# Block products of the MLPs in another order, modulation sums in PSUM, weights two passes ahead

## The reference

```python
h = rmsnorm(x, norm_mlp[l]) * (1.0 + sc2) + sh2
ff = square(relu(h @ mlp_w1[l])) @ mlp_w2[l]      # 1024 -> 4096 -> 1024
x = x + g2 * ff
```

## Time and profile before

| | |
|---|---|
| median of 3 runs | 2931.09 us |
| profiled execution | 2930.64 us, span 2928.8 us |
| busy: TensorE, VectorE, POOL, ScalarE | 88%, 65%, 47%, 38% |
| mean granted TensorE clock | 0.943 |
| layer 0's MLP, passes 0 to 30 | 605.1 to 1530.2 us |
| layer 1's MLP, passes 32 to 62 | 2033.8 to 2870.9 us |

### The profile page before, as it was taken

How to read it: one execution, slowest core, us unless ns; L and a number is a source line. 1 busy time by engine, 2 the same in 40 slices (tenths; PEclk the granted TensorE clock), 3 DMA queues, 4 the chain that set the end, 5 groups by cost and what they waited for, 6 DMA issues and landing times. The chain is left out here.

```text
span 2928.8 us, 42150 instructions
## 1 busy us (share of the span) xinstructions
PE 2571.2 (88%) x13962; PEld 2462.9 (84%) x13962; DVE 1915.5 (65%) x2837; ACT 1113.4 (38%) x1884; POOL 1372.3 (47%) x907
## 2 busy tenths in 40 slices
PE   8999998978887896799997988878899996799997
PEld 4999998978787896799996877678899996699997
DVE  5876877367677764777775677765643443777775
ACT  5332333243333334333334454423444433433334
POOL 1211211244554454777772322334466664577772
PEclk9999999989999998899998999989999998899998
DMA  6422223214434435433332111132222235433332
GB/s 234 134 85 58 74 81 114 95 38 162 153 138 145 141 138 201 139 117 116 116 115 97 36 36 36 32 111 77 78 106 90 112 116 196 150 122 113 115 119 94
DMA packets 245983, 324.24 MB, mean 111 GB/s; under 512 B 14710, under 2 KB 221046, under 8 KB 239863
## 3 DMA queue, kind: packets, MB, share of 16 engines
q1 hardware_dynamic: 242436, 303.31, 31.0%
q10 hardware_dynamic: 3442, 19.65, 1.7%
HBM read 242.16 MB, written 80.75 MB: 110 GB/s over the span
## 5 line engine op out<-in xcount | busy, mean ns | idle before, releaser
L1086 PE MATMUL psum<-early_hi,unit_hi 128*128 128x384 f32 (+1 forms) x1408 | 507.0, 360 | 145.1 <-DVE part_x L1876 57.5
L1086 PE MATMUL psum<-late_hi,unit_hi 128*128 128x384 f32 x1408 | 485.1, 345 | 80.2 <-DVE x L1978 58.9
L787 POOL TENSOR_TENSOR unit_lo<-wide_raw,unit_hi 128x512 fp32r<-128x512 f32 x256 | 383.3, 1501 | 290.3 <-ACT unit_hi L1391 290.3
L1086 PE MATMUL psum<-early_lo,unit_hi 128*128 128x384 f32 (+1 forms) x1408 | 497.2, 353 | 0.0
L1086 PE MATMUL psum<-early_hi,unit_lo 128*128 128x384 f32 (+1 forms) x1408 | 496.2, 352 | 0.0
L1086 PE MATMUL psum<-late_lo,unit_hi 128*128 128x384 f32 x1408 | 480.6, 341 | 0.0
L1086 PE MATMUL psum<-late_hi,unit_lo 128*128 128x384 f32 x1408 | 480.3, 341 | 0.0
L1086 PEld LDWEIGHTS psum<-early_hi,unit_hi 128*128 128x128 f32 x1408 | 282.4, 201 | 163.2 <-DVE part_x L1876 62.0
L787 POOL TENSOR_TENSOR unit_lo<-unit_sum_s,unit_hi 128x512 fp32r<-128x512 f32 x256 | 375.0, 1475 | 61.1 <-ACT unit_hi L1391 60.9
L761 POOL CAST w_hi<-w_raw 128x1024 fp32r<-128x1024 f32 x56 | 58.6, 1046 | 706.2 <-DMA w_raw<-in_ab_w_in 260.0
L1391 ACT ACTIVATE unit_hi<-unit_sum_s 128x512 fp32r<-128x512 f32 x256 | 156.7, 625 | 559.1 <-POOL unit_sum_s L806 367.9
(11 more groups left out here) (285 smaller groups left out, 4227.0 us busy)
## 6 DMA issues: line engine op xcount, KB each, us to landing
wide_raw<-in_mlp_w SPq DMA_DIRECT2D x120, 512.0 KB, 4.4
hidden<-stage SPq DMA_DIRECT2D x32, 1728.0 KB, 7.4
late_raw<-hidden SPq DMA_DIRECT2D x270, 192.0 KB, 2.4
wide_mod<-in_mod_w SPq DMA_DIRECT2D x96, 256.0 KB, 2.8
mod_raw<-in_mod_w SPq DMA_DIRECT2D x64, 256.0 KB, 2.9
late_raw<-hidden SPq DMA_DIRECT2D x18, 768.0 KB, 7.4
w_raw<-in_ab_w_in SPq DMA_DIRECT2D x24, 512.0 KB, 4.5
x_spill<-x ACTq DMA_DIRECT2D x2, 4608.0 KB, 13.0
```

Of the source, the lines that this page charges most:

```text
L787: pool.tensor_tensor(unit_lo[u][:], raw, unit_hi[u][:].bitcast(F32), ALU.subtract).then_inc(unit_ready, 1)
L1086: mm = pe.matmul(bank(dst, 0, width), w[:, n, :], v[:, slot, 0:width], start=(start and n == 0 and w is unit_hi[u] and v is hi), stop=(sto ...
```

## The change

The change does this, in both MLPs:

- Order of a pass on TensorE: B11, PL1, PL1, B21, PL2, PL2, T4, then T2, T1, T3, B22; all units that are blocks of the weights come first, the sums S2, S1, S3, S4 after them. PSUM banks are dealt out anew. PL1's first product waits for all eight evacuations of the pass before.
- The sums of weight blocks get scratch tiles of their own, and POOL's two waits for `step_done` go.
- `wide_free` waits only until A22 of the pass before is cut, and SP issues weights two passes ahead; in the second half between the refills of T4 and T2.
- Modulation: two batches of 256 columns per pass, four slots of `wide_mod`, sums in PSUM (`ssq_psum`), copied to SBUF at the end of a batch. Batch 0 stands as a whole ahead of the first evacuation, batch 1 is spread between the others; TensorE's columns stand behind the third and the seventh product.
- At the turn all `late_part` of the fills stand in `second`, none in `first`; the fills' order is PL1, PL2, B11, B21, T4, T2, T1, T3, B22. ScalarE rectifies and squares in place in `stage`.

```diff
-A11, A21, S2, S1, S3, A12, A22, S4 = range(8)
-B11, PL1, T2, T1, T3, B21, PL2, T4, B22 = range(9)
+A11, A21, A12, A22, S2, S1, S3, S4 = range(8)
+B11, PL1, B21, PL2, T4, T2, T1, T3, B22 = range(9)
-MOD_WIDE = 4
+MOD_WIDE = 2
+MOD_PASSES = 12
+MOD_OPS = 2 * KT + 1
+MOD_START = MOD_OPS + 8
...
+        unit_sum = {u: sb(f"unit_sum_{u}", [PAIRS, P], tables_at + 2048 * n) for n, u in enumerate((S1, S2, S3, S4))}
+        wide_mod = sb("wide_mod", [4, MOD_WIDE * P], t_at[0] + 13824)
+        BANK = {"a": (0, 0), "f": (0, 1), "c": (0, 2), "d": (1, 0), "b": (1, 1), "e": (1, 2)}
+        wide_total = ssq_psum[:].rearrange("p (n m) -> p n m", n=2)
...
                 def wide_free(q):
-                    sp.wait_ge(unit_ready, q.n(STEPS, STEPS * R))
+                    sp.wait_ge(unit_ready, q.n(STEPS, STEPS * (R - 1) + A22 + 1))
...
                 def first(q, half):          # SP
                     if with_mods:
-                        mods(q, range(2))
-                    wide_free(q.next())
-                    wide_first(q.next())
+                        mods(q, 0, range(4))
                     if q.j or q.i is not None:
                         store(q.last(), 1 - half)
                     if with_mods:
-                        mods(q, range(2, KT))
+                        mods(q, 0, range(4, KT))
+                        mods(q, 1, range(4))
+                    wide_free(q.plus(2))
+                    wide_first(q.plus(2))
+                    if with_mods:
+                        mods(q, 1, range(4, KT))
...
                 def second(p):               # SP
-                        wide_free(p.next().plus(HALF_PASSES))
-                        wide_second(p.next())
-                        refill(p)
+                    for e in (B11, PL1, B21, PL2, T4):
+                        refill(p, e)
+                    if p.i is not None or p.j < HALF_PASSES - 2:
+                        wide_free(p.plus(2 + HALF_PASSES))
+                        wide_second(p.plus(2))
+                    for e in (T2, T1, T3, B22):
+                        refill(p, e)
...
                     on(B11, "a", A11).then_inc(first_done, 1)        # TensorE
-                    pe.wait_ge(evacuated, q.n(EVACS, V - EVACS + 5))
+                    pe.wait_ge(evacuated, q.n(EVACS, V))
                     on(PL1, "e", A11, stop=False, width=plain).then_inc(step_done, 1)
...
                     unit_part(l, nq, A21)                            # ScalarE, first
+                    act.wait_ge(scaled, q.n(4, 4 * H + 1))
+                    act.wait_ge(evacuated, q.n(EVACS, V + 2))
+                    rectify(b11, 0)
+                    rectify(pl1, 0, True)
+                    square_part(q, 1, b11)
+                    square_part(q, 2, pl1)
+                    unit_part(l, nq, A12)
+                    act.wait_ge(evacuated, q.n(EVACS, V + 3))
+                    rectify(pl2, 1, True)
+                    unit_part(l, nq, A22)
...
+                                op = dve.scalar_tensor_tensor(out=wide_total[:, n, :], in0=wide_mod[:, k % 4, :], scalar=c,
+                                                              in1=wide_total[:, n, :], op0=ALU.mult, op1=ALU.add)
+                    if k == KT - 1:                                  # VectorE, mods
+                        dve.wait_ge(mod_used, q.n(2 * MOD_WIDE, MODS + MOD_WIDE * (batch - 2)))
+                        dve.wait_ge(wide_mod_step, q.n(2 * MOD_OPS, B + 2 * KT))
+                        dve.tensor_copy(wide_sum[:], wide_total).then_inc(wide_mod_step, 1)
...
                     if q.j or q.i is not None:                       # VectorE, first
                         sums(q.last(), 1 - half)
                     if with_mods:
+                        mods(q, 0, range(KT))
...
+                    dve.wait_ge(step_done, q.n(STEPS, S + 3))
+                    dve.tensor_tensor(b11, bank("b"), part_p[:], ALU.add).then_inc(evacuated, 1)
+                    dve.tensor_copy(bias[:, 0, :], bank("e", CH, CH + 2))
+                    dve.tensor_tensor(pl1, bank("e"), parts[2], ALU.mult).then_inc(evacuated, 1)
...
+                    joined(q, l, 4)
+                        mods(q, 1, range(2, 4))
+                    joined(q, l, 5)
+                        mods(q, 1, range(4, 6))
...
                     joined(q, l, 5)                                  # VectorE, second
                     add(part_v[:], m1, CH, 2 * CH, 0).then_inc(x_added, 1)
                     add(part_v[:], m2, CH, 2 * CH, 0).then_inc(x_added, 1)
                         new_part(p, T2)
                     dve.wait_ge(step_done, q.n(STEPS, S + 7))
+                    add(bank("b"), m2, CH, 2 * CH, 0)
+                    add(bank("b"), m2, 0, CH, 0).then_inc(evacuated, 1)
                     add(bank("d"), m2, 0, CH, 0).then_inc(evacuated, 1)
+                        new_part(p, T1)
                     dve.wait_ge(step_done, q.n(STEPS, S + 8))
+                    add(bank("e"), m1, CH, 2 * CH, 0).then_inc(evacuated, 1)
```

More of the change, by code:

```diff
@@ L1430, in first @@
-                    rectify(out_e, 0, True)
-                    square_part(q, 1, part_p, stage[half][:, B11, :])
-                    square_part(q, 2, out_e, stage[half][:, PL1, :])
-                    if fills:
-                        late_part(FILL.index(T2), T2)
-                    unit_part(l, nq, A12)
-                    act.wait_ge(evacuated, q.n(EVACS, V + 6))
-                    rectify(part_w, 1)
-                    rectify(out_f, 1, True)
-                    act.wait_ge(scaled, q.n(4, 4 * H + 3))
@@ L1440, in first @@
[L1440 to L1446 removed]
+                    act.wait_ge(scaled, q.n(4, 4 * H + 2))
+                    rectify(b22, 1)
+                    act.wait_ge(scaled, q.n(4, 4 * H + 3))
@@ L1915, in sums, with first @@
                     dve.tensor_tensor(t4, b21, t2, ALU.subtract).then_inc(parts_summed, 1)
-                def first(q, half, opened=False, fills=False):
-                    with_mods = l == 0 and (q.i is not None)
-                    if not opened:
+                def first(q, half):
+                    with_mods = l == 0 and q.i is not None
+                    b11, pl1, pl2, b21, b22 = (stage[half][:, e, :] for e in (B11, PL1, PL2, B21, B22))
+                    if q.j or q.i is not None:
@@ L1932, in first @@
-                    if not opened:
-                        joined(q, l, 3)
-                    dve.wait_ge(evacuated, q.n(EVACS, V + 3))
-                    scale(part_w, 1).then_inc(scaled, 1)
-                    if fills:
-                        late_part(FILL.index(B11), B11)
-                    if with_mods:
-                        mods(q, range(3, 6))
-                    dve.wait_ge(step_done, q.n(STEPS, S + 6))
-                    dve.tensor_tensor(part_p[:], bank("a"), part_p[:], ALU.add).then_inc(evacuated, 1)
@@ new lines, in second @@
+                    add(bank("b"), m1, 0, CH, 0).then_inc(evacuated, 1)
+                    add_plain("e", m1).then_inc(evacuated, 1)
+                    if opened:
+                        for e in (T3, B22):
+                            late_part(FILL.index(e), e)
+                        new_part(p, B11)
+                        new_part(p, PL1)
+                    if ended:
+                        low(0)
+                    dve.wait_ge(step_done, q.n(STEPS, S + 4))
+                    add_plain("f", m2).then_inc(evacuated, 1)
```

441 lines of the change are left out of this document (196 added, 245 removed).

## The result

Timed side by side, the kernel before takes 2932.55 us (median of 4 runs, 2926.3 to 2938.51) and the changed kernel 2997.82 (4 runs, 2990.38 to 2999.54). The ratio is 1.0218, 95% interval 1.019 to 1.0246: **slower by 65 us**. The forecast was slower, 2972, inside 2885 to 3040. The profiled execution of the changed kernel took 2999.54 us with a span of 2997.7, which is 68.9 more than the span of before.

What follows compares the result with a forecast made beforehand. TensorE, by far the busiest engine, was taken as the bound, losing time in waits for VectorE. Terms +60, +64, -25, -46, -8 and -4 make +41: 2972 us, slower, range 2885 to 3040 (forecast's own 2945 to 3000).

Steps and rivals of the forecast that it cites:

- Modulation passes: Passes 1 to 12: one chain of waits makes each 38.5 us instead of 33.5, +60 us, bounds +30 and +90.
- the four sums: Modulation pass, VectorE's sums of the pass before: one at 1.4 us and three at about 0.5, done at 8.9.
- The prices of loads: Modulation pass: load 4 behind the hidden store takes 6.7 us, as before; 6.9 taken from the store's issue.
- Multiply-adds in PSUM: Modulation passes, VectorE: 28 of 256 columns at a step of 0.39 us, 10.9 us; arithmetic saves 1 to 2 us.
- Second half: 28 second-half passes: late T2 refill and PL1's wait for the last add make 26.3 us instead of 24.0, +64 us.
- Rival 2: Second half: clock falls in every pass, stall about 3 us, 1.7 us per slow stretch, +48 more, 3020 us; chance 0.2.
- Layer 1's first half: Passes without modulation: weights freed at A22 end POOL's wait, 11 passes go from 25.76 to 23.5 us, -25 us.
- The turns: Between MLP halves: pass 15 runs at 23.3 us, PL1 of pass 17 starts at about 72; -46 us for both layers.
- Small ones: Openings -8 us, last passes -4, and PSUM banks, scratch tiles and POOL's dropped waits 0.
- Openings: Start of each MLP: T3 and B22 stand behind three reciprocals that start some 7 us sooner, -4 us each.
- The last passes: Their 5 us wait before T4 goes, but squares and gains on ScalarE hide most of it: -4 us.
- the pass of 41: Modulation passes: upper bound of 41 us a pass, +90 us.

Runs made afterwards that it cites:

- six such edits: Changed kernel with second batch's loads, second half's refills and A21 first, two sum buffers, GpSimd behind VectorE's sums, store behind first batch's loads: 2717.62 us, ratio 0.9269.

## Why the prediction was right, and where its sizes were off

**Modulation passes, +91.5 where +60 stood (and +9.4 in pass 13).** The chain is the forecast one, link by link, in pass 8: wait for the columns, sums, load 4 behind the store, load 4 behind the wide weights, last evacuation. From the last evacuation's end the links measured (forecast): copy done 7.7 (6.0), sums done 13.2 (8.9), load 4 there 20.6 (16.0), PL1 evacuated 25.5 (20.8), second load 4 there 37.4 (32.5), last evacuation 42.1 (37.2, and 38.5 with the clock). The **step that was mis-sized is the four sums**, 5.6 us where 2.9 stood: the prediction took three of them at about 0.5 and only one at the 1.4 of the earlier trace rows, whose mean of nine was the warning. The run with GpSimd behind them gave 2.1 us for the four and 3.1 us a pass back. The copy's wait is 1.7 us longer, since TensorE's first product of PL1 ran at the low clock (3.8 us where 2.1 stood, the second 2.1); the forecast added 1.3 for this at the end, so only 0.4 of it is a miss. With 2.7 for the sums and 0.5 for the loads and evacuations it makes the 3.6 us between 38.5 and 42.1. The prices of loads held: 6.24 us from issue to landing (6.7), and 4.5 for the issue at 977.19 behind two wide loads. Moving either load took away its share, 49 and 81 us. Pass 13 carries no modulation sums of its own, but TensorE's wait at its start (9.1 us) is for the evacuations of pass 12; the prediction charged 12 passes and forgot that the last one's lateness is seen in the next.

**Multiply-adds in PSUM.** The forecast step was 0.39, and the timeline shows eight in 3.23 us, 0.39 each. The 1030 ns of the earlier trace rows for the old form is a mix: in the trace of the kernel before, the multiply-adds of 128x512 take 0.74 us alone and 1.75 (median) beside GpSimd's work. On the Trainium skill's rule ("VectorE: DVE Perf Modes", section "The TRN2 errata"), by which a PSUM source costs more per instruction: its figure for 28 instructions (11.0 us) agrees with the step of 0.39, but the form in SBUF has the same duration and the same step (0.48 and 0.39 us), so no surcharge is seen for the multiply-add, and where one is seen, at the plain multiplication of 256 columns and the copy of 512, it is 0.13 and 0.26 us, in proportion to the columns and not a fixed cost. Another section of that page of the Trainium skill, "The perf-mode tier table (the rule you actually need)", fits that better: it gives plain fp32 copies and tensor_scalar a double rate between SBUF tiles.

**Second half, +57.6 where +59 stood for these 26 passes.** Right in kind: T2's refill behind the wide loads, and PL1 waiting for the last addition. From PL1's start in pass 27 the refill has landed at 20.9 us (20.3 forecast), is cast at 21.5 (20.9), the last addition ends at 25.5 and PL1 of pass 28 starts at 25.6. The prediction's own terms add up to 24.9 to 25.9 there, and not to the 25.3 to 26.2 that it writes. Its 26.3, said to hold some slow clock, is just 0.1 above these. The measured mean is 26.25, of which the slow clock is 0.9 (14 stretches at 1.7 us over 26 passes), so that the total came so close is partly luck. The two edits split it. With the refills first a pass is 24.8, with A21 first it is 23.4 and 23.3 even with the refills behind the weights, so the wait in front of PL1's first product is what the other causes feed into.

**Rival 2 came in part.** Of 26 second-half passes 12 had a stretch at 1.2 GHz, 3.4 or 6.8 us long; clock 0.95 and 0.98 in the stage rows. The columns of this pair of passes (27 and 28, stalls of 2.0 and 2.5 us in front of PL1) show the difference:

```profile
1545.14:1570.23 25.09, 23.39 (x133) 23.06 (x133) 16.36 (x24) 8.81 (x18) 16.42 (x12) 1.00 0.36 111
1570.23:1597.40 27.17, 24.95 (x134) 24.63 (x133) 16.74 (x25) 9.76 (x20) 16.42 (x12) 0.94 0.34 105
```

With stalls of 2.0 to 2.8 us 14 passes kept their clock and 8 lost it, with 3.2 to 3.7 all four lost it, and with 1.7 to 1.8 in all 26 (refills first) none did. So the rule in the Trainium skill ("TensorE: Matmul & The Clock Gate", section "HAM oscillation — how this bites in real kernels") that a wait in each tile can throttle anew each time holds here in about half of the passes; the forecast had "at times".

**Layer 1's first half, -29.4 where -25 stood.** Passes 36 to 46 run at 23.27 with TensorE busy all of the time (the stage row from 2255.11: 256.00 us of 256.00).

**The turns, -45.9 where -46 stood: the number is in part luck.** Pass 15's products run without a wait, as forecast, but the low part of B11, forecast at 26 us from the start of pass 15, is done at 35.2, and TensorE waits 11.9 us for it in front of pass 16. The first fill is issued at 16.2 (14 forecast); ScalarE begins to cast only at 27.5, behind its squares of pass 15, and VectorE makes B11's low as its third. B22, named as the likely longest wait, is not waited for at all (low part at 55.9, TensorE there at 59.2). The second wait, before PL1 of pass 17, is the forecast one: it ends at 76.0 in layer 0 and 76.1 in layer 1, where 72 stood. So the steps give 49 us in place of the 57 that the prediction added up, and another 3 go in what is left of passes 17 and 49; what brought the number home is the 11 us that it had taken off by judgement.

```profile
1238.69 0.66 PE L1082 MATMUL psum<-late_hi,unit_hi 128*128 128x384 f32 x1 [11.91 <-DVE late_lo L1943]
...
1279.34 0.69 PE L1082 MATMUL psum<-late_hi,unit_hi 128*128 128x384 f32 x1 [9.93 <-DVE x L1955]
```

No experiment undid these two parts of the change, so their causes are read from the traces alone.

**Small ones.** Openings: passes 0 and 32 cost 0.7 and 1.3 us more where -4 each was forecast. The reciprocals begin 29.3 us into pass 0 where they began 32.8, but the third one waits for ScalarE and they end only 2.0 us earlier; TensorE's product of T1 stands behind a matmul of the norm that waits 6.0 us for ScalarE (3.8 before), and the one ahead of T2 waits 2.2 for VectorE. The prediction had looked at VectorE's order alone. The last passes and what follows give -18.1 where -4 stood. The products of passes 31 and 63 take 24.9 us each where they took 30.8 and 31.1, with a wait of 5.2 us before T4: that is 12 of the 18, so next to nothing of this wait was hidden behind ScalarE, where the prediction had most of it hidden. Another 6.8 us lie between the start of layer 1's mixer and pass 32; their cause is open. That banks and scratch tiles cost nothing was not tested by itself either.

Against the bounds: the pass of 41 that gave +90 was the upper end for the modulation passes, and 91.5 with 9.4 more behind it lies outside. So the sum missed by 28 us: +31.5 and +9.4 in the modulation passes and the one behind them, +12 in the openings, -6 in the second half, -4 in layer 1's first half, -14 at the ends of the layers. The misses are +53 and some -25 us, so a part of the closeness is that they cancel.

## What to carry to other kernels

When an engine's queue holds loads with different deadlines in one fixed order, ask for each load which semaphore the instruction ahead of it waits for, and which engine's late work that is: here two orders of issue were worth 49 and 81 us, and 35 in the second half, with no instruction added. If a wait guards one of two output banks, do the work of the free bank first; this one exchange of lines was worth 101 us, more than what the whole change had lost. A chain that closes around a pass gave nothing back for VectorE's cheaper multiply-adds, but every wait in it could be taken away singly, and the gains of six such edits came to 280 us, four fifths of the 345 that they make one by one.

## What the runs showed of the hardware

- GpSimd beside VectorE slows VectorE's operations with two SBUF sources by a factor of three (0.55 to 1.6 us for 128x384, and 1.51 for a multiply-add of 128x256 in which GpSimd had just begun), GpSimd's own by a quarter (1.29 to 1.60 us for 128x512). The same operations with one source in PSUM keep their 0.55 and 0.48 us beside it: in layer 0's MLP of the changed kernel 78 multiply-adds into PSUM ran beside GpSimd, in 0.47 to 0.48 us each. Holding GpSimd back made the kernel 36 us faster. The Trainium skill, "SBUF — State Buffer", section "Who interferes with whom", states it: a VectorE operation with two SBUF inputs contends with a GpSimd one that reads SBUF, and the later of the two is blocked until the first is through. The runs agree: the multiply-add that began 0.09 us behind GpSimd's operation of about 1.3 us took 1.51 instead of 0.48.
- A load of 128 KB issued 0.8 us behind a store of 1728 KB lands with it, 6.2 us after its issue, and in 2.1 us ahead of it. Its lateness is that of the transfer in front: it moved to whichever load was next.
- A stall of 1.7 to 1.8 us in each pass cost no granted clock in 26 passes, while one of 2.0 to 2.8 cost a stretch of 3.4 us at 1.2 GHz in 8 of 22. In layer 0's second half the refill that came 2.6 us sooner shortened a pass by 1.9 us, of which only part is the stall (2.0 to 3.7 before, 1.8 after).
